# Squares and row-scaled products kept in PSUM during two residual additions of an encoder step

## The reference

```python
x = x + mixed @ w_o                        # mixed: two attention outputs, each RMS-normed, 512 + 512 wide
q = rms_norm(x, g_mem) @ w_mq              # 4 heads x 128
p = softmax(q k_mem^T * MEM_SCALE); o = p @ v_mem
x = x + o @ w_mo
hf = rms_norm(x, g_ffn)
x = x + (silu(hf @ w_gate) * (hf @ w_up)) @ w_down
```

## Time and profile before

| | |
|---|---|
| time, median of 3 runs | 894.79 us (893.72 to 897.13) |
| the profiled execution | 897.35 us, its span 895.6 us |
| PE busy | 848.6 us, 95% |
| DVE busy | 551.0 us, 62% |
| ACT busy | 400.5 us, 45% |
| POOL busy | 365.5 us, 41% |
| mean granted clock of PE | 0.982 |
| chain that ended last | PE 71%, DVE 6%, issue 3%, ACT 1% |

### The profile page before, as it was taken

The page is one execution under the profiler, slowest core; times in us unless marked ns, Lnnn a source line. Parts: engine busy times, 40 slices in busy tenths (PEclk is TensorE's granted clock), DMA queues, the critical chain, the costliest instruction groups (busy, mean ns, idle before and its releaser), DMA issues.

```text
span 895.6 us, 16042 instructions
## 1 busy us (share of the span) xinstructions
PE 848.6 (95%) x5930; PEld 784.8 (88%) x5930; DVE 551.0 (62%) x875; ACT 400.5 (45%) x736; POOL 365.5 (41%) x212
## 2 busy tenths in 40 slices
PE   6999999899999899989899989999999999999994
PEld 6988988677887799978589989999999998999994
DVE  5256354656555854863546899999999989312213
ACT  6443454535556533444535455555555555222110
POOL 2644854634422544662129233333333335433410
PEclk9999999999999999999999999999999999999997
DMA  7332421100105323333012212222222233223102
GB/s 244 109 111 69 156 80 44 56 1 19 48 1 172 113 65 91 120 112 97 0 45 98 94 49 94 94 94 93 94 94 94 93 127 90 87 85 89 42 1 106
DMA packets 25239, 75.49 MB, mean 84 GB/s; under 512 B 2896, under 2 KB 5272, under 8 KB 25048
## 3 DMA queue, kind: packets, MB, share of 16 engines
q1 hardware_dynamic: 25184, 74.74, 26.2%
HBM read 68.20 MB, written 6.53 MB: 83 GB/s over the span
## 4 chain that ended last, share of the span: by engine, by line
PE 71%; DVE 6%; issue 3%; ACT 1%; POOL 0%; DVEq 0%; ACTq 0%
PE ps L452 21%; PE ps L453 20%; PE ps L454 20%; PE ps L619 3%; PE ps L603 1%; PE ps L855 1%; PE ps L470 1%; PE ps L478 1%; DVE xb L2022 1%; DVE hlo L1753 1%; DVE tl L1863 1%; PE ps L625 0%; PE ps L588 0%; PE ps L582 0%; DVE sqacc L1760 0%
## 5 line engine op out<-in xcount | busy, mean ns | idle before, releaser
L452 PE MATMUL ps<-hhi,whi 128*128 128x288 f32 x896 | 270.0, 301 | 18.8 <-DVE hlo L1455 6.6
L453 PE MATMUL ps<-hhi,wlo 128*128 128x288 f32 x896 | 266.1, 297 | 0.0
L454 PE MATMUL ps<-hlo,whi 128*128 128x288 f32 x800 | 237.8, 297 | 0.0
L2033 POOL TENSOR_TENSOR wlo<-wraw,whi 128x1024 fp32r<-128x1024 f32 (+1 forms) x48 | 115.3, 2407 | 212.2 <-ACT whi L980 203.1
L452 PEld LDWEIGHTS ps<-hhi,whi 128*128 128x128 f32 x896 | 170.3, 190 | 22.2 <-issue 10.5
L980 ACT ACTIVATE whi<-wraw 128x1024 fp32r<-128x1024 f32 (+3 forms) x138 | 114.8, 838 | 137.3 <-PE ps L454 119.8
L453 PEld LDWEIGHTS ps<-hhi,wlo 128*128 128x128 f32 x896 | 169.9, 190 | 0.1
L454 PEld LDWEIGHTS ps<-hlo,whi 128*128 128x128 f32 x800 | 151.5, 189 | 0.0
L2179 POOL TENSOR_TENSOR wlo<-wraw,whi 128x512 fp32r<-128x512 f32 x60 | 77.3, 1302 | 155.2 <-ACT whi L980 155.2
L454 PE MATMUL ps<-hidlo,whi 128*128 128x288 f32 x352 | 103.9, 295 | 0.0
L2193 POOL TENSOR_TENSOR wlo<-wraw,whi 128x1024 fp32r<-128x1024 f32 (+1 forms) x24 | 56.8, 2372 | 77.6 <-ACT whi L980 77.6
(11 more groups left out here) (277 smaller groups left out, 1870.8 us busy)
## 6 DMA issues: line engine op xcount, KB each, us to landing
wraw<-w_ff SPq DMA_DIRECT2D x44, 512.0 KB, 4.1
wraw<-w_front SPq DMA_DIRECT2D x41, 512.0 KB, 3.6
wraw<-w_down SPq DMA_DIRECT2D x16, 512.0 KB, 3.6
wraw<-w_down SPq DMA_DIRECT2D x8, 384.0 KB, 3.3
wraw<-w_front SPq DMA_DIRECT2D x7, 384.0 KB, 3.6
xs<-x_t SPq DMA_DIRECT2D x8, 288.0 KB, 6.1
xa<-x_t SPq DMA_DIRECT2D x8, 288.0 KB, 5.1
out_y<-xb SPq DMA_DIRECT2D x8, 288.0 KB, 2.3
```

What stands on the lines that cost most here:

```text
L452: nc.tensor.matmul(out, lh, rh, start=start, stop=False)
L453: nc.tensor.matmul(out, ll, rh, start=False, stop=False)
L454: return nc.tensor.matmul(out, lh, rl, start=False, stop=stop)
L2033: g.tensor_tensor(wlo[:, b % 3, 0:n], wraw[:, b % 2, 0:n], f(whi[:, b % 3, 0:n]), ALU.subtract).then_inc(f_lo, 1)
```

## The change

In both stages ScalarE writes the square of tile m (m > 0) into the PSUM pair that the tile's product came from, in place of `tmp2`, and the square sum reads it there. In the first stage VectorE also writes the product with the row factors back into its pair instead of `evt`, and the addition into `xa` reads it there. A pair is therefore in use until the square sum of its tile (for tile 0: its square), and PE's waits for a pair name those counters.

```diff
@@ -762,7 +762,7 @@
                 elif m == 2:
                     pe.wait_ge(s_mkev, 4)
                 else:
-                    pe.wait_ge(s_wmt, m - 2)
+                    pe.wait_ge(r_acc, m - 3) if m > 3 else pe.wait_ge(r_sq, 1)
                 mm = wide(PAIR_WOM[m], 4, lambda k: [front(b, lo, 8, 128)[:, 4 * (m % 2) + k, :] for lo in (0, 1)], x1, k0=4,
                           wait_k=(lambda k: pe.wait_ge(s_olo, 5 + k)) if m == 0 else None)
                 mm.then_inc(f_used[b % 3] if m % 2 else s_gdone, 1)
@@ -801,14 +801,14 @@
                 if k1 == 8:
                     mm.then_inc(f_used[b % 3], 1)
 
-            pe.wait_ge(s_wmt, 7)
+            pe.wait_ge(r_acc, 6)
             query(0, 0, 8, lambda k: pe.wait_ge(r_lo, k + 1))
             pe.wait_ge(r_acc, 7)
             columns(2, sqacc).then_inc(n_col, 1)
             memory_values(3)
             pe.wait_ge(n_rc, 4)
             spread(rows2(2), small[:, S_RCC:S_RCC + 5], range(TT)).then_inc(n_row, 1)
-            pe.wait_ge(s_wmt, 8)
+            pe.wait_ge(r_acc, 7)
             query(1, 0, 8)
 
             def mscores(s):
@@ -896,7 +896,7 @@
                 elif m == 3:
                     pe.wait_ge(m_rbs, MH)
                 else:
-                    pe.wait_ge(r_x, 8 + m - 3)
+                    pe.wait_ge(r_acc, 7 + m - 4) if m > 4 else pe.wait_ge(r_sq, 9)
                 mm = wide(pair, 4, lambda k: [front(b, lo, 8, 128)[:, 4 * (m % 2) + k, :] for lo in (0, 1)], (mohi, molo),
                           wait_k=(lambda k: pe.wait_ge(m_olo, k + 1)) if m == 0 else None)
                 mm.then_inc(f_used[b % 3] if m % 2 else s_gdone, 1)
@@ -907,7 +907,7 @@
 
             for c in range(4):
                 pe.wait_ge(g_lo, c + 1)
-                pe.wait_ge(r_x, 8 + (5, 6, 8, 7)[c])
+                pe.wait_ge(r_acc, 7 + (4, 5, 7, 6)[c])
                 wide(c, KT, lambda k: [ffw(c, lo, KT, 128)[:, k, :] for lo in (0, 1)], x1,
                      wait_k=(lambda k: pe.wait_ge(r_lo, 8 + k + 1)) if c == 0 else None).then_inc(g_used, 1)
                 if c == 0:
@@ -1204,7 +1204,7 @@
                     activation(sqacc[:, 0:T], xa[:, 0, :], ACT.Square).then_inc(r_sq, 1)
                 else:
                     need(act, r_acc, m - 2)
-                    activation(tmp2[:, m % 2, :], xa[:, m, :], ACT.Square).then_inc(r_sq, 1)
+                    activation(two(PAIR_WOM[m]), halves(xa[:, m, :]), ACT.Square).then_inc(r_sq, 1)
                 if m < 4:
                     activation(hhi[:, m, :], xa[:, m, :], scale=gains[:, G_MEM + m:G_MEM + m + 1]).then_inc(r_hi, 1)
                 if m == 1:
@@ -1278,7 +1278,7 @@
                     activation(sqacc[:, 0:T], xb[:, 0, :], ACT.Square).then_inc(r_sq, 1)
                 else:
                     need(act, r_acc, 7 + m - 2)
-                    activation(tmp2[:, m % 2, :], xb[:, m, :], ACT.Square).then_inc(r_sq, 1)
+                    activation(two(PAIR_MO[m]), halves(xb[:, m, :]), ACT.Square).then_inc(r_sq, 1)
                 activation(hhi[:, m, :], xb[:, m, :], scale=gains[:, G_FFN + m:G_FFN + m + 1]).then_inc(r_hi, 1)
                 if m == 1:
                     split(48)
@@ -1753,11 +1753,11 @@
                 v.scalar_tensor_tensor(hlo[:, m, :], xa[:, m, :], gain(G_MEM, m), f(hhi[:, m, :]),
                                        ALU.mult, ALU.subtract).then_inc(r_lo, 1)
 
-            def square_sum(m, at, count):
+            def square_sum(m, at, count, pair):
 
                 dve.wait_ge(r_sq, at + m + 1)
                 need(dve, r_acc, count + m - 1)
-                v.tensor_tensor(sqacc[:, 0:T], sqacc[:, 0:T], tmp2[:, m % 2, :], ALU.add).then_inc(r_acc, 1)
+                v.tensor_tensor(halves(sqacc[:, 0:T]), halves(sqacc[:, 0:T]), two(pair), ALU.add).then_inc(r_acc, 1)
 
             for m in range(8):
                 if m % 2:
@@ -1766,16 +1766,16 @@
                     dve.wait_ge(s_gdone, 3 + m // 2)
                 if m > 0:
                     dve.wait_ge(r_x, m)
-                v.tensor_tensor(halves(evt[:, :]), two(PAIR_WOM[m]), halves(rstd[:, :]), ALU.mult).then_inc(s_wmt, 1)
+                v.tensor_tensor(two(PAIR_WOM[m]), two(PAIR_WOM[m]), halves(rstd[:, :]), ALU.mult).then_inc(s_wmt, 1)
                 dve.wait_ge(s_wmt, m + 1)
-                v.tensor_tensor(xa[:, m, :], xa[:, m, :], evt[:, :], ALU.add).then_inc(r_x, 1)
+                v.tensor_tensor(halves(xa[:, m, :]), halves(xa[:, m, :]), two(PAIR_WOM[m]), ALU.add).then_inc(r_x, 1)
                 if m == 1:
                     memory_key(3)
                 if 1 <= m < 5:
                     low2(m - 1)
                 if m >= 2:
-                    square_sum(m - 1, 0, 0)
-            square_sum(7, 0, 0)
+                    square_sum(m - 1, 0, 0, PAIR_WOM[m - 1])
+            square_sum(7, 0, 0, PAIR_WOM[7])
             for m in range(4, 8):
                 low2(m)
 
@@ -1848,9 +1848,9 @@
                 if m >= 1:
                     low3(m - 1)
                 if m >= 2:
-                    square_sum(m - 1, 8, 7)
+                    square_sum(m - 1, 8, 7, PAIR_MO[m - 1])
             low3(7)
-            square_sum(7, 8, 7)
+            square_sum(7, 8, 7, PAIR_MO[7])
             def t_sum(n, a, b):
 
                 dve.wait_ge(x_hf, KT)
```

## The result

| | median us | lowest to highest | runs |
|---|---|---|---|
| before, beside it | 897.13 | 893.72 to 900.39 | 5 |
| after | 889.95 | 888.76 to 892.14 | 5 |

The ratio is 0.9928, with a 95% interval of 0.9899 to 0.9956: 0.72% faster, where 0.49% was forecast. A second measurement gave 890.82 against 897.87, ratio 0.9927 (0.9907 to 0.9947); one of its 17 executions of before took 1641 us, far outside the rest, and is left out of that ratio. The profiled execution took 892.14 us, its span 890.3; the trace of before has 895.6.

A forecast was written before the change was run, and what follows sets the result against it. PE's waits for VectorE's low tiles at the first memory query, 3.9 us in all, were taken as the bound. One term, 4.4 us, took the span from 895.6 to 891.2 and the median from 894.79 to 890.4; range 888.9 to 894.6.

The forecast's parts named there:

- The lock waits go: First stage, VectorE: additions and square sums lose their waits for GpSimd, up to 2.21 us each, falling to about 0.75.
- The new forms: Both stages: instructions with PSUM operands take about as long as in SBUF, all within 0.1 us over the tail.
- The 65 ns of the errata: Additions reading PSUM: the skill estimates 65 ns more each; the forecast held the trace disagrees and the gain stays 4.4.
- What is late next: First memory query: low tiles end at 385.3, PE no longer waits, column sums start at 388.30 instead of 392.72; gain 4.4 us.
- The race: End of first stage: the fourth low tile starts at 384.5, ahead of GpSimd's next instruction at 385.17; the closest race.
- The waits: Waits that the change adds on PE in both stages; each was forecast to be covered, with time to spare.
- (a): First query: PE newly waits for square sum 6, ending at 381.45 before the start at 381.83; covered by 0.38 us.
- (b): First stage: w_o's tile 6 waits for square sum 3, ending at 371.84, with 0.74 us to spare.
- (c): Second stage: the last w_mo tile waits for square sum 3, with about 2 us to spare.
- Rival (E): Both stages: PSUM traffic slows PE's products by a quarter, 8.3 us, giving 898.7, slower than before; chance 0.08.
- The second stage gives nothing: Second stage: VectorE saves 2.2 us on a square sum, but PE is busy throughout and takes none of it.
- rival (D): Memory attention: with its gaps gone PE gets half the missing granted clock, 1.5 us more, giving 888.9; chance 0.12.

The follow-up runs named there:

- the short GpSimd: Kernel before with GpSimd's low parts of weight blocks 37 to 42 cut to 64 columns and two memory-key subtractions replaced by memsets: 891.47 us, ratio 0.9928.
- The additions alone: Kernel before with only the first stage's row-factor product and addition into xa going through PSUM, squares staying in tmp2: 894.84 against 898.09 us, ratio 0.9951.
- the squares alone: Kernel before with only the first stage's squares going through PSUM, evt staying in SBUF: 890.96 against 898.09 us, ratio 0.9926.
- The filled gaps: Kernel before with 16 and 12 unread extra products in PE's gaps ahead of the query's k = 4 and k = 7: 896.17 against 898.21 us, ratio 0.9983.

## Why the prediction was right, and where it was short

**Right, by its steps.** It forecast events at the times of the trace of before; after starts tile 0 0.77 us earlier (346.76 against 347.53), so 0.77 is taken off here.
- *The lock waits go*: the maxima of L1771 and L1760 are 756 and 753 ns, and shortening GpSimd alone does the same.
- *The new forms*: the addition from PSUM 754, bound 751; the product into PSUM 766 in the middle, where the same line into SBUF had 757 in the trace of before, +0.01 as put. ScalarE's square into PSUM 656 and 648 ns, where the upper bound 0.68 was taken and no gain:

```profile
L980 ACT ACTIVATE ps<-xa 128x576 f32<-128x576 f32 x7 | 4.6, 656 | 17.3 <-DVE xa L1771 17.3
L980 ACT ACTIVATE ps<-xb 128x576 f32<-128x576 f32 x7 | 4.5, 648 | 5.5 <-DVE xb L1847 5.5
```

- *The 65 ns of the errata* (the Trainium skill, "VectorE: DVE Perf Modes", section on the TRN2 errata) don't show: 754 with the PSUM operand, 757 at best without it.
- *What is late next*: nothing. The last low tile ended at 384.43 (forecast 385.3 - 0.77 = 384.5), the column sums started at 387.49 (388.30 - 0.77 = 387.5).
- *The race*: GpSimd's next at 384.41 (385.17 - 0.77 = 384.4), the fourth low tile under way. GpSimd's batch started at 373.15, 1.1 us ahead of the forecast (375.04 - 0.77 = 374.27), and ended at 380.42, clear of the low tiles. The forecast had left a wait out: low tile 3, which keeps its two SBUF operands, took 1.85 in place of 2.95, since GpSimd was done sooner, and so all behind it on VectorE moved 1.1 more (before, then after):

```profile
368.21 2.95 DVE L1753 SCALAR_TENSOR_TENSOR hlo<-xa,gains,hhi 128x576 fp32r<-128x576 f32 x1
```

```profile
367.43 1.85 DVE L1753 SCALAR_TENSOR_TENSOR hlo<-xa,gains,hhi 128x576 fp32r<-128x576 f32 x1
```

- *The waits*: (a), (b) and (c) stayed covered; the query starts 0.23 us behind the product before it, the pace of that kind. Rival (E), PE slowed by the traffic in PSUM, falls with the pace: 24 products from 381.05 to 384.27, 0.134 each.
- *The second stage gives nothing*: 0.9991 alone.

**Short by a term.** The sum held one term, the 4.4 us of PE's idle time, and that was measured as 4.46 in the stage. The median fell by 7.2, because the sum lacked the clock's term. The step that failed is the one that put rival (D) aside: it placed the clock's part in the memory attention and argued "the clock is 1.00 right through the gaps". In the trace of before it is, and behind them too; in the three other executions with both gaps it is 0.50 behind them, and from tile 0's product to the query's eviction they take 3.2 to 3.4 us more. The part that (D) did name, up to 1.5 us in the attention, is there as well, with 1.2 in the mean.

Over 42 timed executions of before the mean clock lay between 0.973 and 0.989, and a line through them has 0.56 us for each 0.001, with a spread of 0.6 us and 1.6 at most. Read off at one clock, 0.982, before is 896.9, after 891.6, the first stage alone 891.8, and the short GpSimd 892.3: 4.6 to 5.4 us, near the 4.4 of the code. The additions alone are 894.8 and the squares alone 893.2, so 2.2 and 3.8 us, near the 2.45 and 3.70 of the stage. The filled gaps, by that line, are 897.0: before's own value, so by it their whole gain is clock. The line is a correlation; it doesn't say what moves the clock. The mean clock was 0.980 for before and 0.984 for after, which is the remaining 2 us. Up to 0.9 us between 4.46 and 5.4 stays open; the line is not good for less.

The measured 889.95 lies in the range (888.9 to 894.6), near its low end; the ratio laid on the 894.79 us from which the forecast started gives 888.4, 0.5 us under it. The mechanism and its size in the stage were right. The chances leaned too far to "same": the sum stood on the line of 0.5%, and the clock's part, on the side of faster, had been given 12%.

## What to carry to other kernels

Where VectorE's rows of one shape differ in length and the long ones end behind GpSimd's, put one of the two SBUF operands into PSUM, starting with the instruction whose delay pushes later work into GpSimd's next one. An idle time of PE can cost more than its length: read several executions for the clock behind it, since one that shows 1.00 proves nothing, and where the gap can't be closed try useless products in it. Before costing both halves of an edit, ask which of the waits the next stage can afford; here the squares alone gave 3.70 of the 4.46 us.

## What the hardware showed that was not expected

- The same instructions with the same gaps ran at 1.00 in one execution and at 0.50 for some 7 to 10 us in three others. The cost was 3.2 to 3.4 us each time, from tile 0's product to the first query's eviction.
- 28 products that nobody reads went with 2.0 us less by the medians (1.5 by the ratio), and 12 in another place with 3.4 us less by the ratios, of which the trace ties 1.6 to them.
- ScalarE's square of 576 columns is about 30 ns shorter into PSUM (656, 648) than into SBUF (686 in the first stage of before, 682 for the squares of xb).
